# First layer's mixer in two halves of 256 tokens, the second half and no modulation chunk beside the first quarter of gathers

## The chip, the core and the metric

The kernel runs on one core of a Trainium2 chip. The core has TensorE (PE, matrix products into PSUM), VectorE (DVE), ScalarE (ACT), GpSimd (POOL) and SyncE (SP), which run their own instruction streams and meet at semaphores, and 16 DMA engines that serve several queues. Two queues matter here: SP's, which brings weights, and POOL's, which brings gathered rows. The metric is the device time of one launch in microseconds (us), as a median of runs.

## What is computed

A network of three layers over 512 tokens of width 1024, all in float32. Cut to what matters for the change:

```python
c_act = silu(c)
for l in range(2):
    mod = c_act @ ada_w[l] + ada_b[l]                     # 1024 x 6144
    sh1, sc1, g1, sh2, sc2, g2 = jnp.split(mod, 6, axis=-1)
    hn = modulate(rms_norm(h, norm_mix_g[l]), sh1, sc1)   # xn * (1 + scale) + shift
    mix = hgrn2_mixer(hn, ...) if l == 0 else stick_breaking_mixer(hn, k_sh, v_sh, ...)
    h = h + g1 * mix
    hn = modulate(rms_norm(h, norm_ffn_g[l]), sh2, sc2)
    h = h + g2 * peer_ffn(hn, ...)
    if l == 0:                                            # k_sh, v_sh; c_act @ kv_ada_w: 1024 x 2048
        k_sh, v_sh = shared_kv(h, c_act, ...)
h = rms_norm(h, final_norm_g)
# then second_block: convolution and windowed attention, then a mixture of 32 experts
```

`hgrn2_mixer` projects to q, f, i and g (1024 x 4096 weights), keeps a state of 128 x 128 in each of 8 heads, which goes from chunk to chunk of 16 tokens in order, and projects back with `w_out`. `peer_ffn` scores 2 x 128 subkeys in 4 heads, takes the best 64 experts of each token, and for each of them reads a row of 1024 numbers of `u` (a dot with the token gives the weight) and one of `v` (summed with these weights): 512 x 64 x 2 rows of 4 KB in each of the two layers.

## The kernel before

Tokens lie in four tiles of 128 (TT = 4). The program is a list of phases; all engines meet between two of them (`enter`, `leave`). The first seven phases hold the first layer up to its expert scores, for all four tiles at a time: `setup_*`, the norm, `hgrn_in_*` (projections), `hgrn_scan_*` (four levels of masked scores, then the state from tile to tile), `hgrn_out_norm_*`, the output projection with the second norm, and `peer_query`.

Then comes one long phase, `rows_pe`, `rows_act`, `rows_dve`, `rows_pool`. It has four quarters (w = 0 to 3) of 64 steps. A quarter serves two tiles: in steps 0 to 31 DVE takes the dots of the `u` rows (`dots_dve`, L943, four rows a step), in steps 32 to 63 PE sums the `v` rows (`sum_pe`, L1034). POOL gathers the rows (`gather_pool`, L931: 128 rows of 4 KB in one DMA) into a ring of 6 pairs of buffers, so it is at most three steps ahead. Beside it the quarters w = 1 and 2 run the second layer's mixer for half of the tokens each, as generators (`block_pe`, `block_act`, `block_dve`), of which every engine takes one piece at fixed steps (`seg_step`); w = 3 does so with the first half of the second block. Quarter w = 0 has no such block, but the last 18 of the modulation chunks. `route_dve` (the selection of 64 experts) of the odd tile runs in steps 1 to 11 of its own quarter, that of the next quarter's even tile late in the quarter before; that of tile 0 runs ahead of the first step.

A modulation chunk is a product of `c_act` (a column) with 1024 x 512 weights, 2 MB: there are 12 for each layer and 4 for `shared_kv`, 28 in all. `mod_parts_pe` (L242) multiplies it on PE in four groups of 32 columns, ACT copies the partial sums, `mod_total_pe` (L273, L275) adds bias and partial sums over all 128 partitions, ACT writes the result. Four chunks run in setup, six beside the projections of `hgrn_in_pe`, which load into a buffer of their own (`MOD_SIDE`), and 18 in the first quarter (`MOD_STEP`).

Weights of 1024 x 512 (2 MB) come on SP's queue through two slots, w0 and w1, in the order of `stream`. POOL also writes 13 MB of zeros to `x_slots`, which the last block needs (`zero_slots`), at the start of `hgrn_in`.

```python
MOD_EARLY = 10
MOD_FIRST = 4
MOD_STEP = {2 + 3 * j: j for j in range(len(MODS[1]))}
ROWS_AT, TURN_AT = (2, 16), (26, 40)
```

## Time and profile before

| | us |
|---|---|
| median of 3 runs | 3250.94 (3245.38 to 3251.22) |
| the profiled execution | 3263.15 |
| its span | 3261.6 |
| first-layer phases, to the copy ahead of the first dots | 0 to 569.3 |
| first quarter of gathers (w = 0) | 569.3 to 1017.9 |
| second quarter (w = 1) | 1017.9 to 1457.9 |
| third quarter (w = 2) | 1457.9 to 1906.9 |
| fourth quarter (w = 3) | 1906.9 to 2364.5 |
| the rest of the second block, and the experts | 2364.5 to 3261.6 |

The bounds of the quarters are the starts of the copies at L959, of tiles 0, 2, 4 and 6. The profile shows busy times of the engines, which don't add up to the span, since they overlap; what an engine waits for decides. PE was busy for 2242.1 us (69%), DVE for 1368.6 (42%), POOL for 1089.2 (33%), ACT for 482.3 (15%), and the DMA engines moved 963.65 MB, 295 GB/s over the span.

### The profile page before, as it was taken

Reading aid. Unit: us, or ns where it says so; the run is one execution under the profiler, and the core shown is the slowest. Engines: PE = TensorE matmul, PEld = TensorE weight load, DVE = VectorE, ACT = ScalarE, POOL = GpSimd, SP = SyncE. Lnnn points to the kernel's source line nnn. Section 1 sums busy time; section 2 is a strip of 40 time slices with the busy share of each in tenths; the row PEclk is TensorE's granted clock in tenths of the full one; section 3 lists DMA queues with packets and bytes.
Section 4 is the critical chain, followed back from the end, with each engine's and each line's share of the span. In section 5 each row is a group of like instructions: output and inputs, shape, how many; then the busy total and the mean of one; then the engine's idle time right before and its main releaser. Section 6 shows DMA issues by size and latency. Waiting matters only on the chain.

```text
span 3261.6 us, 27740 instructions
## 1 busy us (share of the span) xinstructions
PE 2242.1 (69%) x10176; PEld 1180.6 (36%) x10176; DVE 1368.6 (42%) x3001; ACT 482.3 (15%) x817; POOL 1089.2 (33%) x1220
## 2 busy tenths in 40 slices
PE   6999796323555657848577626667788758888884
PEld 2444543111113343405463315533377423333331
DVE  1032523785305962149661369683136211111112
ACT  2121211000001032101151010020022101111111
POOL 2000000564555546564555555466400010000001
PEclk8999898555777867968789758788899769898997
DMA  7542011999998989998989989999824278989995
GB/s 282 204 150 78 14 52 58 386 405 379 403 403 327 405 342 340 350 376 342 365 303 366 344 324 358 373 326 365 316 103 144 99 277 339 391 349 399 396 394 193
DMA packets 273994, 963.65 MB, mean 295 GB/s; under 512 B 31760, under 2 KB 36880, under 8 KB 261582
## 3 DMA queue, kind: packets, MB, share of 16 engines
q0 software_dynamic: 159728, 577.32, 46.8%
q1 hardware_dynamic: 102920, 378.61, 30.6%
q10 hardware_dynamic: 11222, 6.03, 0.7%
q8 instruction: 82, 1.34, 0.2%
q14 instruction: 42, 0.34, 0.0%
HBM read 933.30 MB, written 28.57 MB: 295 GB/s over the span
## 4 chain that ended last, share of the span: by engine, by line
PE 50%; DMA 12%; issue 11%; DVE 10%; another core or an unknown queue 6%; POOL 6%; ACT 4%; POOLq 0%; DVEq 0%; SPq 0%; ACTq 0%
PE psum L194 25%; PE psum L2080 8%; DMA arena<-in_peer_v_dram,arena 6%; POOL arena L931 5%; PE psum L2094 5%; PE psum L1034 4%; DMA arena<-in_peer_u_dram,arena 2%; DVE arena L943 2%; PE psum L1140 1%; DMA arena<-in_sb_w_q_dram 1%; DMA arena<-in_kv_w_dram 1%; PE psum L1430 1%; PE psum L242 1%; DMA arena<-in_ada_w_dram 1%
## 5 line engine op out<-in xcount | busy, mean ns | idle before, releaser
L194 PE MATMUL psum<-arena 128*128 128x256 f32 (+3 forms) x3144 | 974.1, 470 | 92.7 <-issue 35.5
L194 PEld LDWEIGHTS psum<-arena 128*128 128x128 f32 x3144 | 606.8, 198 | 469.5 <-issue 386.9
L931 POOL DMA_INDIRECT arena<-in_peer_u_dram,arena x512 | 485.6, 949 | 589.8 <-DVE arena L943 247.4
L931 POOL DMA_INDIRECT arena<-in_peer_v_dram,arena x512 | 502.8, 982 | 385.7 <-PE psum L1034 200.9
L943 DVE CUSTOM_DVE_ANT_0 arena<-arena,psum 128x1024 f32<-128x1024 f32 x512 | 594.1, 1217 | 44.0 <-DMA arena<-in_peer_u_dram,arena 29.4
L1034 PE MATMUL psum<-arena 128*32 128x512 f32 x2048 | 320.5, 757 | 222.9 <-DMA arena<-in_peer_v_dram,arena 188.8
L2080 PE MATMUL psum<-arena 128*64 128x512 f32 x1088 | 253.8, 621 | 67.0 <-issue 65.8
L1034 PEld LDWEIGHTS psum<-arena 128*32 128x32 f32 x2048 | 68.7, 126 | 424.8 <-issue 420.9
L2094 PE MATMUL psum<-arena 128*64 128x512 f32 x544 | 161.4, 748 | 17.6 <-DVE arena L2130 17.6
L2080 PEld LDWEIGHTS psum<-arena 128*64 128x64 f32 x1088 | 80.5, 142 | 239.3 <-issue 237.9
L2126 DVE TENSOR_TENSOR arena<-arena,psum 64x512 f32<-64x512 f32 x34 | 23.5, 692 | 313.6 <-ACT arena L2107 313.6
L2140 POOL DMA_DIRECT2D arena<-x_slots x37 | 19.1, 517 | 381.1 <-DVE arena L2114 373.6
L984 PE MATMUL psum<-arena 128*32 128x16 f32 x512 | 18.9, 203 | 156.0 <-issue 83.6
L242 PE MATMUL psum<-arena 128*32 128x512 f32 x448 | 76.9, 819 | 44.4 <-DMA arena<-in_kv_ada_w_dram 26.9
L1020 DVE TENSOR_TENSOR arena<-arena 128x512 f32<-128x512 f32 x32 | 21.8, 691 | 189.5 <-PE psum L1034 157.9
L2019 POOL DMA_INDIRECT x_slots<-arena x8 | 7.7, 967 | 275.0 <-DVEq L180 272.9
L1650 DVE SCALAR_TENSOR_TENSOR arena<-arena 128x256 f32<-128x256 f32 x240 | 97.4, 480 | 0.0
L2107 ACT ACTIVATE arena<-psum 64x512 f32<-64x512 f32 x34 | 20.0, 588 | 513.9 <-PE psum L2080 513.9
L1045 DVE TENSOR_TENSOR psum<-psum,arena 128x1024 f32<-128x1024 f32 x8 | 9.9, 1233 | 199.2 <-PE psum L1034 113.9
L1140 PE MATMUL psum<-arena 128*128 128x256 f32 (+1 forms) x208 | 56.2, 440 | 53.6 <-DVE arena L1283 39.9
L2156 POOL DMA_DIRECT2D x_slots<-arena x68 | 36.7, 540 | 149.2 <-DVE arena L2134 147.6
L2094 PEld LDWEIGHTS psum<-arena 128*64 128x64 f32 x544 | 45.0, 173 | 108.8 <-issue 86.5
(331 smaller groups left out, 2038.1 us busy)
## 6 DMA issues: line engine op xcount, KB each, us to landing
arena<-in_w_gate_dram SPq DMA_DIRECT2D x32, 2048.0 KB, 20.4
arena<-in_w_up_dram SPq DMA_DIRECT2D x32, 2048.0 KB, 9.9
arena<-in_w_down_dram SPq DMA_DIRECT2D x32, 2048.0 KB, 14.4
arena<-in_ada_w_dram SPq DMA_DIRECT2D x24, 2048.0 KB, 7.9
arena<-in_w_in_dram SPq DMA_DIRECT2D x14, 2048.0 KB
arena<-in_hgrn_w_in_dram SPq DMA_DIRECT2D x8, 2048.0 KB
arena<-in_kv_w_dram SPq DMA_DIRECT2D x8, 2048.0 KB
x_slots<-arena POOLq DMA_DIRECT2D x25, 512.0 KB, 13.9
```

Of the source, the lines that this page charges most:

```text
L194: last = pe.matmul(o, lhsT=lhs(k), rhs=rhs(k), start=start and k == 0, stop=stop and k == n - 1)
L242: last = pe.matmul(bank(MOD_BANKS[l][0], 0, 512, parts=(32 * q, 32)), lhsT=C_COLS(k0 + q), rhs=w[:, k0 + q, :], start=k0 == 0, stop=k0 == ...
L931: pool.indirect_dma_start(RING(n, k), None, (U_TAB, V_TAB)[v], bass.IndirectOffsetOnAxis(ap=at, axis=0))\
L943: last = dve.tensor_tensor_reduce(out=row, in0=row, in1=bank(XB0, 0, D), scale=1.0, scalar=0.0, op0=ALU.mult, op1=ALU.add, accum_out=par_s ...
L1034: last = pe.matmul(bank(ACC + half, 0, 512, parts=(32 * g, 32)), lhsT=mem("t", D + (s // 4 % 2) * 512 + (g * GR + s % 4) * 32, 32), rhs=RI ...
L1140: last = pe.matmul(bank(ZB(h), o + w - min(w, wm), min(w, wm)), lhsT=mem("negtri" if m == n else "negones", 0, P), rhs=AW(hf, h, om, wm), ...
L1430: last = pe.matmul(bank(b, p * 256, 256, parts=(64 * a, 64)), lhsT=wslot(i)[:, k, a * 256 + (2 * b + p) * 64:a * 256 + (2 * b + p) * 64 + 64],
L1650: ins = dve.scalar_tensor_tensor(Y2(hf, c), CV(c, 256 * hf + i, 256), CCOL(c, i), Y2(hf, c), ALU.mult, ALU.add)
L2080: last = pe.matmul(bank(2, 0, FF, parts=half(m)), lhsT=XBT[:, k, :], rhs=EW(e, m)[:, k, :], start=k == 0, stop=k == KD - 1, skip_group_che ...
L2094: last = pe.matmul(bank(4, 0, 512, parts=half(n)), lhsT=HT[:, k, :], rhs=EW(e, 2)[:, k, n * 512:(n + 1) * 512], start=k == 0, stop=k == NF ...
L2126: dve.tensor_tensor(HM, SG, bank(2, 0, FF, parts=half(1)), ALU.mult).then_inc(sem("hm"), 1)
L2156: pool.dma_start(y_slots[bass.ds(g * SLOTS, SLOTS), m * 512:(m + 1) * 512], mem("w1", 0, D // 2, parts=half(m)))\
```

## The change

The seven phases are gone: after `setup_*` there is the long phase alone. The first layer's mixer, the second norm and the expert scores become a generator of 36 pieces (`first_pe`, `first_act`, `first_dve`), which works on two tiles. Half 0 (tiles 0 and 1) runs ahead of the quarters, half 1 (tiles 2 and 3) beside the first quarter at the steps of `first_step`. All 28 chunks run beside half 0: four ahead of its first piece, and one after each of its first 24 pieces on PE. POOL loads them (`mods_pool`) into two buffers, in r5 and r6, and puts one block of zeros for `x_slots` behind each. A chunk that is needed as a row over the width (g1, sh2, sc2, g2 of both layers: 16 chunks) goes by way of DRAM: DVE adds its bias (`mod_out_dve`), POOL stores 2 KB of it, waits until they have landed, and later reads the row back for all partitions. POOL does this in one stream with the loads. The partial sums of a chunk are copied by DVE (`mod_acc_dve`), no longer by ACT, and are added on PE with a weight of a single column (L654) or, for the other 12 chunks, in four products with one column each (L657). The weights of the first layer's mixer are read twice, once for each half. The biases and gains that are needed as columns are loaded in setup: 72 columns of 128 numbers, 4 bytes a piece. The expert scores of tiles 2 and 3 are there only at step 51 of the first quarter, so the selection for tile 2 moves from step 36 to step 53. The quarters w = 1, 2 and 3 keep their work; w = 1 gains four loads of rows (`rows_1_act`), and the window constants move on POOL to the start of w = 2.

```diff
-        add("mod0", [w_cols(ada[0], 512 * j) for j in range(MOD_FIRST)])
-        add("hgrn_in", [w_cols(win[0], D * part + 512 * c) for part in (1, 0, 2, 3) for c in range(2)])
-        add("hgrn_out", [w_cols(A["hgrn_w_out"][0], 512 * c) for c in range(2)])
-        add("peer_q0", [w_cols(A["peer_w_q"][0], 512 * c) for c in range(2)])
-        add("mod1", [w_cols(ada[0], 512 * j) for j in range(MOD_EARLY, 12)] + [w_cols(kva, 512 * j) for j in range(4)] + [w_cols(ada[1], 512 * j) for j in range(12)])
+        for hf in range(2):
+            add(f"hgrn_in{hf}", [w_cols(win[0], D * part + 512 * c) for part in (1, 0, 2, 3) for c in range(2)])
+            add(f"hgrn_out{hf}", [w_cols(A["hgrn_w_out"][0], 512 * c) for c in range(2)])
+            add(f"peer_q0{hf}", [w_cols(A["peer_w_q"][0], 512 * c) for c in range(2)])
+            add(f"keys0{hf}", [A["peer_subkeys"][0].rearrange("h p n d -> n (h p) d")])
...
+            for at, n, row in ((0, 16, A["kv_ada_b"]), (16, 16, A["ada_b"][1, 0:2 * D]), (64, 16, A["ada_b"][0, 0:2 * D]),
+                               (32, 8, A["kv_norm_g"]), (40, 8, A["norm_mix_g"][1]), (80, 8, A["norm_mix_g"][0])):
+                act.dma_start(mem("tiny", at, n), row.rearrange("(k p) -> p k", p=P), allow_slow_non_contiguous=True)\
+                    .then_inc(sem("cols_in"), 16)
+            act.dma_start(mem("r0", 0, 2 * D, parts=(0, 1)), A["norm_ffn_g"].rearrange("(a l) n -> a (l n)", a=1))\
+                .then_inc(sem("cols_in"), 16)
...
+        def mods_pool(pool):
+
+            for j in range(2, NCHUNK + 4):
+                i = j - 4
+                if i in ROW_NO:
+                    r = rows_before(i) + 1
+                    pool.wait_ge(sem("mod_row"), r)
+                    pool.dma_start(mod_rows[ROW_NO[i] // 2:ROW_NO[i] // 2 + 1, 512 * (i % 2):512 * (i % 2) + 512], MOD_ROW(i))\
+                        .then_inc(sem("mod_stored"), 16)
+                    pool.wait_ge(sem("mod_stored"), 16 * r)
+                    n = ROW_NAMES[ROW_NO[i] // 2]
+                    if i % 2 and n[-2:] == "_0":
+                        pool.dma_start(mod(MOD0[n[:-2]]), mod_rows[ROW_NO[i] // 2:ROW_NO[i] // 2 + 1, :].broadcast_to([P, D]))\
+                            .then_inc(sem("row_g2" if n == "g2_0" else "row_in"), 16)
+                if j < NCHUNK:
+                    pool.wait_ge(sem("mod_acc"), j - 1)
+                    mod_load(pool, j)
+                    if j in ROW_NO:
+                        pool.dma_start(MOD_ROW(j), mod_source(j)[1]).then_inc(sem(f"mod_bias{j % 4}"), 16)
+                zero_slots(pool, j - 2)
...
+        def mod_acc_dve(dve, j, link):
+
+            if j >= 2:
+                dve.wait_ge(sem("mod_mm"), j - 1)
+            if BY_PE[j]:
+                dve.wait_ge(sem("mod_part"), sum(BY_PE[:j + 1]))
+                dve.tensor_copy(MOD_ACC(j), bank(6 + j % 2)).then_inc(sem("mod_acc"), 1)
+                return
...
+
+            if not BY_PE[j]:
+                return
+            mod_arrived(pe, j)
+            if j >= 2:
+                pe.wait_ge(sem("mod_acc"), j - 1)
+            for k0 in (0, 4):
+                for q in range(4):
+                    last = pe.matmul(bank(6 + j % 2, 0, 512, parts=(32 * q, 32)), lhsT=C_COLS(k0 + q), rhs=MOD_W(j)[:, k0 + q, :],
+                                     start=k0 == 0, stop=k0 == 4, skip_group_check=True)
+            last.then_inc(sem("mod_part"), 1)
+
...
+        def mod_sum_pe(pe, j):
+
+            pe.wait_ge(sem("mod_acc"), j + 1)
+            if j >= 2:
+                pe.wait_ge(sem("mod_out"), j - 1)
+            over = FIRST_OF_32 if BY_PE[j] else mem("ones", 0, 1)
+            if j in ROW_NO:
+                last = pe.matmul(bank(4 + j % 2, 0, 512, parts=(0, 1)), lhsT=over, rhs=MOD_ACC(j), start=True, stop=True)
+            else:
...
+            first = marks[f"hgrn_in{hf}"]
+            on_act("x7")
+            for i in range(4):
+                project_pe(pe, first, i, lambda k: head("X", k), did)
+                yield
+            for i in range(4):
+                on_act(f"f{i}")
+                project_pe(pe, first + 2, i, lambda k: head("X", k), did)
+                yield
+            for i in range(4):
+                on_act(f"q{i}")
+                by_token_pe(pe, first + 4, i, lambda k, o, n: head("X", k, o, n), did)
+                yield
...
+        first_step = lambda i: (1 if i == 0 else 2 + int((i - 1) * 1.4) if i < 17 else 25 + int((i - 17) * 2.1) if i < 24
+                                else 39 + int((i - 24) * 1.15))
...
-        ROUTES = {(0, 1): (1, 0.9), (0, 2): (36, 0.9), (1, 3): (1, 0.9), (1, 4): (53, 0.5), (2, 5): (1, 0.9), (2, 6): (53, 0.5), (3, 7): (1, 0.9)}
...
+            if w == 0:
+                return sum(first_step(i) == s for i in range(A_SEGS))
+            return sum(seg2_step(i) == s for i in range(SEGS2))
+        ROUTES = {(w, 2 * w + 1): (1, 0.9) for w in range(4)} | {(w, 2 * w + 2): (53, 0.5) for w in range(3)}
...
         def rows_pe(pe):
-            block = iter(())
+            for j in range(4):
+                mod_parts_pe(pe, j)
+                if j:
+                    mod_sum_pe(pe, j - 1)
+            mod_sum_pe(pe, 3)
+            for s, _ in enumerate(first_pe(pe, 0)):
+                if 4 <= s + 4 < NCHUNK:
+                    mod_parts_pe(pe, s + 4)
+                if 4 <= s + 2 < NCHUNK:
+                    mod_sum_pe(pe, s + 2)
             for w in range(TILES // 2):
                 a, b = 2 * w, 2 * w + 1
+                if w == 0:
+                    block = first_pe(pe, 1)
                 if w in (1, 2):
                     block = block_pe(pe, w - 1)
...
-                    if w == 0 and s in MOD_STEP:
-                        mod_pe(pe, 1, [MOD_STEP[s]])
...
         def rows_dve(dve):
             link = linker(dve, "dve")
+            block = first_dve(dve, 0, link)
+            next(block)
+            for j in range(4):
+                mod_acc_dve(dve, j, link)
+                if j:
+                    mod_out_dve(dve, j - 1, link)
+            mod_out_dve(dve, 3, link)
+            for s in range(1, A_SEGS):
+                if s + 3 < NCHUNK:
+                    mod_acc_dve(dve, s + 3, link)
+                if 4 <= s + 1 < NCHUNK:
+                    mod_out_dve(dve, s + 1, link)
+                next(block)
             for _ in route_dve(dve, 0, link):
                 pass
-            block = iter(())
             routes = {}
             for w in range(TILES // 2):
                 a, b = 2 * w, 2 * w + 1
+                if w == 0:
+                    block = first_dve(dve, 1, link)
                 if w in (1, 2):
...
-        phase(**norm(0, mod(MOD0["sc1"]), mod(MOD0["sh1"]), xn_temp, "r0"))
-        phase(hgrn_in_pe, hgrn_in_act, hgrn_in_dve, hgrn_in_pool)
-        phase(hgrn_scan_pe, hgrn_scan_act, hgrn_scan_dve, hgrn_scan_pool)
-        phase(hgrn_out_norm_pe, hgrn_out_norm_act, hgrn_out_norm_dve, window_pool)
-        o0 = out_proj(0, marks["hgrn_out"], lambda k, t: FM("r2", k, t * P, P), KD, MOD0["g1"])
-        n1 = norm(1, mod(MOD0["sc2"]), mod(MOD0["sh2"]), lambda t: mem("r0", t * D, D), "r1", ready=o0["ready"])
-        phase(*both(o0, n1, before=lambda act: peer_load_keys(act, 0)))
-        phase(**peer_query(0))
```

Three places in the order of instructions. The first is PE in the first layer's input projections. Of before, one chunk of the modulation and one 2 MB piece of the projection's weights: L273 and L275 add up the chunk before, L242 multiplies the next, L194 are the projections for 512 tokens.

```order
L273 MATMUL psum<-arena 128x512 [waits mod_bias0,mod_out]
L275 MATMUL psum<-arena 128x512 [waits mod_part]
L242 MATMUL psum<-arena 32x512 [waits mod_side,mod_part]
L242 MATMUL psum<-arena 32x512 x7
L194 MATMUL psum<-arena 128x512 [waits f_out,w_ready0]
L194 MATMUL psum<-arena 128x512 x7
L194 MATMUL psum<-arena 128x512 [waits f_out]
L194 MATMUL psum<-arena 128x512 x7
L194 MATMUL psum<-arena 128x512 [waits f_out]
L194 MATMUL psum<-arena 128x512 x7
L194 MATMUL psum<-arena 128x512 [waits f_out]
L194 MATMUL psum<-arena 128x512 x7
```

Now the same place, with 256 tokens: L188 are the projections, L643 the product of a chunk, L654 its sum over the partitions.

```order
L188 MATMUL psum<-arena 128x256 [waits w_ready0,a_act]
L188 MATMUL psum<-arena 128x256 x15
L643 MATMUL psum<-arena 32x512 [waits mod_acc,mod_w1]
L643 MATMUL psum<-arena 32x512 x7
L654 MATMUL psum<-arena 1x512 [waits mod_out,mod_acc]
L188 MATMUL psum<-arena 128x256 [waits a_act]
L188 MATMUL psum<-arena 128x256 x15
L643 MATMUL psum<-arena 32x512 [waits mod_acc,mod_w0]
L643 MATMUL psum<-arena 32x512 x7
L654 MATMUL psum<-arena 1x512 [waits mod_out,mod_acc]
```

A chunk stood behind 32 products of 512 columns; it stands behind 16 of 256 now. The sum with 128 weight columns and its bias product (two instructions) is one product with one weight column.

The second place is POOL ahead of its first gather. Of before, the zeros for `x_slots` in one go (L1924), and then the constants of the scan.

```order
L1924 DMA x_slots<-arena 128x1024 [waits left_dve,left_pool,left_act,left_pe]
L1924 DMA x_slots<-arena 128x1024 x24
L1924 DMA x_slots<-arena 64x1024
L622 MEMSET arena 128x1024 [waits left_dve,left_pool,left_act,left_pe]
L622 MEMSET arena 128x1024 x3
L623 MEMSET arena 128x384
```

Now the loads of chunks 8 to 11. L588 loads a chunk, L615 its bias, L1904 writes zeros, L604 stores 2 KB of a finished row, L609 reads two such pieces back for all partitions.

```order
L604 DMA mod_rows<-arena 16x1x32 [waits mod_row]
L588 DMA arena<-in_ada_w_dram 128x8x512 [waits mod_acc,mod_stored]
L615 DMA arena<-in_ada_b_dram 1x16x32
L1904 DMA x_slots<-arena 128x1024
L604 DMA mod_rows<-arena 16x1x32 [waits mod_row]
L609 DMA arena<-mod_rows 128x1024 [waits mod_stored]
L588 DMA arena<-in_ada_w_dram 128x8x512 [waits mod_acc]
L615 DMA arena<-in_ada_b_dram 1x16x32
L1904 DMA x_slots<-arena 128x1024
```

A load of a chunk now stands behind the store of the row that was finished two chunks earlier, and behind its landing (`mod_stored`).

The third place is DVE at step 11 of the first quarter. Of before, dots alone (L943, each with the read of its sum).

```order
L943 ISA arena<-arena,psum 128x1024 [waits ring2]
L943 ISA arena 128x1
L943 ISA arena<-arena,psum 128x1024
L943 ISA arena 128x1
L943 ISA arena<-arena,psum 128x1024 [waits ring3]
L943 ISA arena 128x1
L943 ISA arena<-arena,psum 128x1024
L943 ISA arena 128x1
```

Now the prefix sums of the second half of the mixer stand between the dots (L449) of two steps: L934 is 1 - f, L935 the prefix sum, L936 a copy of the last values of each chunk of 16 tokens.

```order
L934 TENSOR_SCALAR arena<-arena 128x512 [waits a_act]
L935 SCALAR_TENSOR_TENSOR arena<-arena 128x512
L936 COPY arena<-arena 128x32 [waits chain_dve]
L934 TENSOR_SCALAR arena<-arena 128x512 [waits a_act]
L935 SCALAR_TENSOR_TENSOR arena<-arena 128x512
L936 COPY arena<-arena 128x32 [waits chain_dve]
L934 TENSOR_SCALAR arena<-arena 128x512 [waits a_act]
L935 SCALAR_TENSOR_TENSOR arena<-arena 128x512
L936 COPY arena<-arena 128x32 [waits chain_dve]
L934 TENSOR_SCALAR arena<-arena 128x512 [waits a_act]
L935 SCALAR_TENSOR_TENSOR arena<-arena 128x512
L936 COPY arena<-arena 128x32 [waits chain_dve]
```

DVE waits there for ACT's logarithms (`a_act`), and the dots behind it wait with it.

## Rows read from the trace of the kernel before

**Rows 1.** windows: us, busy us of PE, PEld, DVE, ACT, POOL, clock, DMA share, GB/s

```profile
0.00:64.50 64.50, 36.59 (x112) 12.64 (x112) 12.31 (x16) 19.44 (x33) 6.91 (x30) 0.79 0.72 251
64.50:314.00 249.50, 246.92 (x632) 103.47 (x632) 44.00 (x72) 46.66 (x81) 13.87 (x26) 0.99 0.44 159
314.00:381.00 67.00, 54.08 (x440) 52.05 (x440) 42.01 (x77) 8.07 (x14) 5.89 (x14) 0.92 0.09 32
381.00:400.00 19.00, 7.11 (x16) 2.96 (x16) 11.60 (x17) 15.91 (x27) 1.48 (x3) 0.80 0.09 28
400.00:473.00 73.00, 65.19 (x160) 30.81 (x160) 21.51 (x29) 11.36 (x21) 0.00 (x0) 0.90 0.19 65
473.00:541.00 68.00, 65.90 (x200) 33.03 (x200) 0.00 (x0) 10.77 (x19) 0.00 (x0) 0.97 0.17 62
541.00:570.00 29.00, 0.44 (x33) 0.47 (x37) 28.01 (x112) 1.77 (x3) 0.00 (x0) 0.58 0.09 19
570.00:790.00 220.00, 57.21 (x327) 28.34 (x319) 180.79 (x378) 8.87 (x19) 131.74 (x140) 0.55 1.02 397
790.00:1018.00 228.00, 131.84 (x752) 37.85 (x752) 38.45 (x130) 13.15 (x24) 120.73 (x127) 0.75 1.01 391
1018.00:1240.00 222.00, 130.00 (x542) 97.23 (x543) 187.00 (x395) 47.47 (x75) 120.98 (x128) 0.75 0.93 355
1240.00:1458.00 218.00, 155.28 (x828) 68.09 (x827) 49.65 (x146) 26.02 (x47) 124.10 (x129) 0.81 0.95 353
```

**Rows 2.** timeline, start: three rows, start us, length us, engine, [idle before <-releaser]

```profile
30.42 0.37 SPq L147 DMA_DIRECT2D arena<-in_ada_w_dram  x1
38.28 3.64 PE L242 MATMUL psum<-arena 128*32 128x512 f32 x16 [2.42 <-DMA arena<-in_ada_w_dram]
53.95 1.94 PE L447 MATMUL psum<-arena 128*128 128x128 f32 x8 [8.02 <-DVE arena L434]
```

**Rows 3.** DMA packets in 3 to 5 us, then in 7 to 13 us

```profile
DMA packets 1787, 0.33 MB, mean 166 GB/s; under 512 B 1628, under 2 KB 1628, under 8 KB 1787
DMA packets 2035, 2.13 MB, mean 355 GB/s; under 512 B 1018, under 2 KB 1018, under 8 KB 2035
```

**Rows 4.** DMA issues: engine, count, KB each, median us from issue to landing

```profile
arena<-in_x_dram ACTq DMA_DIRECT2D x1, 2048.0 KB, 18.9
arena<-in_hgrn_onorm_g_dram ACTq DMA_DIRECT2D x1, 4.0 KB, 11.2
arena<-x_slots POOLq DMA_DIRECT2D x2, 2.0 KB, 4.1
```

**Rows 5.** timeline of PE at the full clock, and beside gathers

```profile
574.43 1.13 PE L275 MATMUL psum<-arena 128*128 128x512 f32 x2
575.49 1.92 PE L242 MATMUL psum<-arena 128*32 128x512 f32 x16
1035.29 27.89 PE L194 MATMUL psum<-arena 128*128 128x256 f32 x128 [0.90 <-ACT arena L1202]
1068.02 29.62 PE L194 MATMUL psum<-arena 128*128 128x512 f32 x64 [4.84 <-DMA arena<-in_kv_w_dram]
```

**Rows 6.** timeline of DVE, first layer: one prefix sum, one tile of one level

```profile
194.90 1.22 DVE L580 TENSOR_TENSOR_SCAN arena<-arena 128x512 f32<-128x512 f32 x1
346.70 1.35 DVE L711 COPY_PREDICATED arena<-arena,psum 128x512 f32<-128x512 int32 x2
347.94 0.68 DVE L715 TENSOR_TENSOR arena<-arena 128x512 f32<-128x512 f32 x1
348.54 0.69 DVE L716 TENSOR_TENSOR arena<-arena 128x512 f32<-128x512 f32 x1
```

**Rows 7.** timeline of DVE: the first selection begins, the first dots

```profile
541.34 1.64 DVE L853 MAX8 arena<-arena 128x8 f32<-128x128 f32 x8 [70.63 <-ACTq L180]
569.33 1.22 DVE L959 COPY psum<-arena 128x1024 f32<-128x1024 f32 x1
577.53 1.22 DVE L943 CUSTOM_DVE_ANT_0 arena<-arena,psum 128x1024 f32<-128x1024 f32 x1 [6.98 <-DMA arena<-in_peer_u_dram,arena]
```

1133 lines of the change are left out of this document (525 added, 608 removed).

## The prediction

> **What bounds the kernel now.** I read the windows by stage first, because the change moves whole stages [rows 1]. Nothing is gathered until 569.3 us. From 64.5 to 314 PE is busy for 246.92 of 249.5 us at a granted clock of 0.99: the input projections are bound by PE at its upper level (2.4 GHz), and DMA is at 0.44. From 314 to 381 the levels of the scan go back and forth between PE and DVE; from 381 to 400 it is the output norm, with ACT; from 400 to 541 the output projection, the second norm and the queries, PE again. DVE alone selects until 570. In the first quarter DMA is the bound in both parts: 397 and 391 GB/s at a share of 1.02 and 1.01. In the second quarter, which has a mixer beside the gathers, DMA has 355 and 353 GB/s, and DVE is busy for 187.00 of 222 us in the part with the dots. So two prices are needed: that of half a mixer with 28 chunks beside it, and that of half a mixer beside the first quarter.
>
> **Setup.** In setup ACT now also loads 72 columns in 4-byte pieces, 72 x 128 = 9,216 of them, behind x, and the phase ends only when they are there. Small pieces alone went at 1,628 in 2 us, 814 per us; beside the 2 MB loads on SP's queue at 1,018 in 6 us, 170 per us [rows 3]. The old columns land at 2.3 + 11.2 = 13.5 us, and x, which had its last byte at 23.2 us behind 512 KB that are gone, about 21.5 [rows 4]. SP now issues four 2 MB loads at once (two chunks, two pieces of weights), 8.4 MB. Beside small pieces 2.13 MB passed in 6 us, 0.35 per us [rows 3], so 2.9 MB by 13.5; beside x, whose pieces are 4 KB against 2, a third of 400 GB/s, 1.0 more by 21.5. The other 4.5 last until about 34.5, and 2,200 small pieces pass beside them. The last 7,000 need 8.6 us. The long phase begins at **43 us**; 35 to 75 are the ends (all small pieces at 814 or at 170 per us).
>
> **First four chunks.** Squares, roots and scaling of the norm take 5 us (before, with one more operation, PE waited for them for 8.02), two products 3.64 each at the lower level of the clock (1.2 GHz), [rows 2]. POOL issues the third load when the first sum is copied, at about 49. A load alone was multiplied 7.9 us after its issue [rows 2]; the fourth lands behind it and behind 512 KB of zeros, 6.6 us later (2.6 MB at 397 GB/s): 63.5. Product, copy, sum and addition bring 71, turns and ACT's copies 75, the fifth product 78. The first projection starts at **78 us**, against 64.5 [rows 1].
>
> **Sixteen projection pieces.** A piece is 16 products of 256 columns: 64 took 27.89 us [rows 5], so 7.0. A chunk adds 1.92 (L242 at the upper level) and a sum of 1.13 (L275) [rows 5], and some 0.4 of starts: 10.5. DMA needs 2.1 MB of chunk, 0.52 of zeros and 1.05 of weights in it, 9.3 us at 397 GB/s. That is close, but hides. For eight of the sixteen, the load of a later chunk stands behind a stored row: 4.1 us for a 2 KB transfer of POOL's queue [rows 4], 7.9 for the load, 1.3 for the zeros ahead of the next store, 13.3 in a row. Part of the latency overlaps with the product's own turn; the ends are 10.5 and 15.9 (SP's 1.05 MB wholly in series), and I take 12.8. Sum: 8 x 10.5 + 8 x 12.8 = 186, to **264 us**. The Trainium skill's page DMA: Bandwidth & Descriptors, section Anatomy of one DMA — SWDGE (gpsimd) path, gives a fixed 2.0 us and 436 GB/s for a transfer of this queue; by it store, load and zeros would last 10.0 us, PE's 10.5 would decide throughout, and the kernel would end some 25 us earlier than I forecast. The 4.1 us above were longer than that.
>
> **Scan and output norm.** One tile of one level was 1.35 us of masks and 2 x 0.6 of decay, 2.56 from one tile to the next [rows 6]; two tiles, the chunk's copy and its addition make 6.2 on DVE, and the first product of the next level is in the open: 8.5. Three pieces of 8.5, 4 for ACT's four gates ahead of them (an estimate: four operations of 512 columns and a change of function), then four pieces whose chunks again stand behind stored rows, 12 each, and 5 in which the output norm (19 us for four tiles, [rows 1]) outlasts the last chunk: 82.5, to **346 us** (ends -15 and +25).
>
> **Tail and selection.** Output projection to scores took 73 + 68 us for four tiles [rows 1]; half of it is 70.5. What doesn't halve is the chain behind the last product (addition, square, root, scaling, turn, copy), the turn of the keys, and two sums of chunks; I take 9.5 for it, 80 in all, with ends at 76 and 92. I add 5 for stretches at the lower level of the clock after the scan. Selection: 28.0 [rows 7]. The copy ahead of the dots comes at 346 + 80 + 5 + 28 = 459, say **460**, in place of 569.3: **-109 us**.
>
> **First quarter.** It loses 18 chunks, and gains half a mixer with its 12 loads of 2 MB and one of 0.5 MB. Steps 0 to 31: the second quarter is the nearest. Its 187.0 us of DVE less some 9 of its own mixer are 178. Half of the first mixer costs on DVE: eight turns of one tile and level at 2.56 less the decay of the first two, 18; prefix sums 4 x 1.45, 6; twenty operations of 512 columns at 0.6, 12; gates, norm, fill and decay products 7 [rows 6]: 43. With 8 us until the first rows are there (569.33 to 577.53, [rows 7]) and 20 of waits for ACT and PE between dots, this is 249, against 221 before. Is PE late? Beside gathers PE waits for weights (4.84 us at 1068.02, [rows 5]); eight pieces of 2 MB at about 17 us each end near 150 us into the quarter, ahead of DVE's step 24. DMA needs 67 MB of rows and some 21 of weights, 222 us at 397 GB/s, so DVE decides by a little. Steps 32 to 63: 218 us as in the second quarter, against 228, since the chunks' 20 MB are gone. Sum **+20 us**; the ends are 0 (all of DVE's extra work in DMA's shadow) and +60 (each of the 36 pieces costs a wait of over a microsecond on top).
>
> **Others.** Four row loads in w = 1, 2.1 MB, 5 us of DMA half hidden: +2. The work that leaves ACT and the single phase bounds are in the numbers above. The quarters w = 2 and 3 and all behind them keep their times.
>
> **Sum.** -109 + 20 + 2 = **-87 us**. Against its own 3263.15 the profiled execution would be 3176; the median lies 12 below it, so I forecast 3250.9 - 87 = **3164 us**.
>
> **Rivals.**
> 1. PE at its lower level through half 0. Before, it was at 0.99 because it hardly waited; beside waits for loads it was 0.75 to 0.81 [rows 1]. If the waits behind stored rows pull it down throughout, a piece is 14.0 + 3.64 + 2.1 = 19.7 us in place of 11.7, +128 in sixteen pieces and +56 in the tail's two projections: the end is about 3350, slower. It decides from about half of the stretch on. Against it: PE will be busy for 10.1 of 10.5 to 12.8 us, 79 to 96%, and where it was busy for 54.08 of 67 and 65.19 of 73 us before, the clock was 0.92 and 0.90. The Trainium skill's page TensorE: Matmul & The Clock Gate, section HAM oscillation — how this bites in real kernels, tells of a kernel that waits for each slice of weights, and in which the clock falls in every wait, so that the next slice starts slow. This has 0.03.
> 2. The first quarter pays for all: DVE's in-order waits empty the ring at each piece, +80 in place of +20, and the time is 3224. DVE was idle for 35 of 222 us in w = 1 [rows 1], which speaks for some of it; that PE is ahead of DVE by the sum above speaks against. It has 0.05 above my range.
> 3. Loads never show (10.5 us throughout, setup at 36), and the quarter's extra DVE work is hidden: -109 - 18 - 16 - 7 with +2 is -148, 3103. Nothing excludes it, but all three terms must be at their ends: 0.08 below my range.
> 4. The half mixer moves work but frees nothing: DVE and DMA in the quarter take what the start gives. For no change the first quarter would have to be 107 us longer than its 448.5 [rows 1], 555 us; its 134 MB of rows and 27 of weights would then pass at 290 GB/s, and no part of a quarter was under 353 [rows 1]. It has 0.02.
>
> **How the numbers follow.** The ends of the terms are setup -8 and +32, pieces -18 and +25, scan -15 and +25, tail -4 and +12, quarter -20 and +40; they hardly fall together, and a root of squares is -32 and +64, of which I take most: **3115 to 3218**, with 0.80 in it. Below it 0.08, above it but faster 0.05, within 0.2% (6.5 us, about what a measurement of this kernel can tell from no change) 0.02, slower 0.05 (rival 1, and 0.02 for a first quarter beyond 555 us). Faster: 0.93.
>
> **What would show it.** In the changed kernel: the first L643 at 43 us, the first L188 at 78, its pieces 10.5 us apart while chunks 5 to 7 and the columns' chunks are loaded and near 13 between; the last masks at about 330; the first gather at 460; DMA under 350 GB/s in steps 0 to 31, and 218 us for the sums. I would be wrong if PE's clock is near 0.5 to 0.8 before 250 us, if the pieces are over 14 us apart, or if the first quarter is over 500 us.

## The result, and the profile after

The changed kernel takes 3141.10 us (median of 4 runs, 3136.08 to 3147.05) where the kernel before took 3251.08 (3245.38 to 3252.50) on the same chip: a ratio of 0.9666, 95% interval 0.9643 to 0.9688, which is 110 us faster. I had forecast 3164 with 3115 to 3218. The profiled execution took 3143.82 us (span 3142.3), 119.3 less than that of before (3263.15); the terms below add up to this number. It is larger than 110 because the profiled execution of before lay 12 us above its median, that of the changed kernel 3 above.

The windows of the changed kernel, cut where a stage of the prediction ends. Columns as in [rows 1].

```profile
0.00:40.50 40.50, 0.00 (x0) 0.00 (x0) 0.54 (x3) 2.98 (x4) 8.69 (x40) 1.00 0.90 260
40.50:76.20 35.70, 25.52 (x128) 12.62 (x128) 5.49 (x14) 9.11 (x16) 7.15 (x10) 0.67 0.77 276
76.20:266.50 190.30, 167.60 (x781) 100.95 (x777) 42.10 (x78) 22.08 (x36) 34.01 (x52) 0.93 0.87 311
266.50:336.10 69.60, 56.33 (x366) 32.55 (x366) 36.29 (x65) 14.07 (x20) 14.50 (x23) 0.88 0.71 259
336.10:412.70 76.60, 65.94 (x252) 43.98 (x252) 13.71 (x20) 12.29 (x28) 1.47 (x3) 0.96 0.27 93
412.70:440.70 28.00, 0.00 (x0) 0.00 (x0) 27.35 (x112) 5.46 (x9) 0.00 (x0) 0.51 0.18 66
440.70:684.00 243.30, 149.50 (x704) 116.48 (x704) 218.17 (x449) 29.10 (x48) 134.61 (x139) 0.80 0.95 362
684.00:896.60 212.60, 160.01 (x872) 74.28 (x872) 59.70 (x165) 28.42 (x49) 121.15 (x126) 0.84 0.96 361
896.60:1338.80 442.20, 289.56 (x1368) 169.58 (x1368) 236.50 (x541) 73.77 (x122) 246.67 (x260) 0.79 0.93 352
1338.80:3142.30 1803.50, 1289.30 (x6152) 713.83 (x6152) 753.22 (x1635) 272.77 (x458) 572.37 (x628) 0.85 0.83 313
```

The starts of two quarters, from the timeline of DVE (the copy ahead of the first dots of tiles 0 and 2; before, 569.33 [rows 7] and 1017.9):

```profile
440.67 1.22 DVE L467 COPY psum<-arena 128x1024 f32<-128x1024 f32 x1
896.56 1.22 DVE L467 COPY psum<-arena 128x1024 f32<-128x1024 f32 x1
```

The copy comes 128.7 us earlier (forecast 109). The first quarter is 455.9 us long where it was 448.5 (+7.4, forecast +20), the second 442.2 where it was 440.0 (+2.2, forecast +2). From there to the end it is 1803.5, and was 1803.7. So -128.7 + 7.4 + 2.2 - 0.2 = -119.3. Nothing behind the second quarter took part.

What [rows 5] showed of the kernel before as one sum (1.13), one chunk's product (1.92) and projections is now this, from the timeline of PE (L188 projections, L643 a chunk, L654 its sum), and beneath it from that of POOL in the same 26 us (L604 stores 2 KB of a row, L588 loads a chunk, L1904 writes zeros):

```profile
104.80 7.17 PE L188 MATMUL psum<-arena 128*128 128x256 f32 x32
111.90 1.92 PE L643 MATMUL psum<-arena 128*32 128x512 f32 x16
113.64 1.02 PE L654 MATMUL psum<-arena 128*1 128x512 f32 x2
114.59 7.17 PE L188 MATMUL psum<-arena 128*128 128x256 f32 x32
127.58 3.64 PE L643 MATMUL psum<-arena 128*32 128x512 f32 x16 [5.81 <-DMA arena<-in_ada_w_dram]
130.99 1.91 PE L654 MATMUL psum<-arena 128*1 128x512 f32 x2
```

```profile
106.47 0.50 POOL L604 DMA_DIRECT2D mod_rows<-arena  x1 [2.56 <-DVE arena L667]
112.32 0.55 POOL L609 DMA_DIRECT2D arena<-mod_rows  x1 [5.34 <-DMA mod_rows<-arena]
112.87 0.98 POOL L588 DMA_DIRECT2D arena<-in_ada_w_dram  x1
113.84 0.51 POOL L615 DMA_DIRECT2D arena<-in_ada_b_dram  x1
114.34 0.57 POOL L1904 DMA_DIRECT2D x_slots<-arena  x1
116.27 0.50 POOL L604 DMA_DIRECT2D mod_rows<-arena  x1 [1.36 <-DVE arena L667]
129.26 0.94 POOL L588 DMA_DIRECT2D arena<-in_ada_w_dram  x1 [12.49 <-DMA mod_rows<-arena]
```

A piece without a wait is 9.79 us from one L188 to the next. With a wait it is 18.25: 5.81 of idle PE, then the chunk in 3.64 and its sum in 1.91 in place of 1.92 and 1.02, since the granted clock has fallen to its lower level (0.50) in the wait. The load that PE waits for was issued at 112.87, behind the store of 106.47, whose landing POOL waited for. The next store (2 KB, 116.27) is waited for 12.49 us: it is in the same queue as the 2 MB load and the 512 KB of zeros issued 2 to 3 us before it, and lands when these have: the zeros 14.5 us after their issue at 114.34, the store 12.7 after its own at 116.27, at 128.8 and 129.0.

### The profile page after: what moved, and what is told of

Same layout as the page of the kernel before. It is cut to its first block, busy times and chain, and to the rows that moved or that the text cites. A ratio compares the mean times of both kernels' runs of the same rounds, so it can differ in the third digit from the quotient of the medians.

```text
span 3142.3 us, 28617 instructions
## 1 busy us (share of the span) xinstructions
PE 2203.8 (70%) x10616; PEld 1264.3 (40%) x10616; DVE 1393.1 (44%) x3073; ACT 470.1 (15%) x789; POOL 1140.6 (36%) x1278
## 4 chain that ended last, share of the span: by engine, by line
PE 43%; DVE 14%; DMA 13%; issue 13%; another core or an unknown queue 7%; POOL 4%; ACT 4%; ACTq 1%; POOLq 0%; PEldq 0%; DVEq 0%; SPq 0%; PEld 0%
PE psum L188 20%; PE psum L2060 8%; DVE arena L449 5%; PE psum L2074 4%; DMA arena<-in_peer_v_dram,arena 4%; PE psum L542 4%; POOL arena L437 4%; DVE arena L1606 2%; DMA arena<-in_ada_w_dram 2%; DMA mod_rows<-arena 1%; PE psum L643 1%; PE psum L1162 1%; DMA arena<-in_kv_w_dram 1%; DMA arena<-in_w_down_dram 1%
## 5 line engine op out<-in xcount | busy, mean ns | idle before, releaser
L188 PE MATMUL psum<-arena 128*128 128x256 f32 (+4 forms) x3656 | 987.1, 430 | 102.4 <-issue 32.6
L188 PEld LDWEIGHTS psum<-arena 128*128 128x128 f32 x3656 | 707.7, 199 | 397.9 <-issue 278.1
L437 POOL DMA_INDIRECT arena<-in_peer_v_dram,arena x512 | 510.4, 997 | 376.3 <-PE psum L542 188.1
L449 DVE CUSTOM_DVE_ANT_0 arena<-arena,psum 128x1024 f32<-128x1024 f32 x512 | 593.2, 1217 | 27.3 <-issue 12.0
L542 PE MATMUL psum<-arena 128*32 128x512 f32 x2048 | 312.0, 740 | 184.3 <-DMA arena<-in_peer_v_dram,arena 153.8
L643 PE MATMUL psum<-arena 128*32 128x512 f32 x448 | 73.0, 785 | 86.4 <-DVEq L174 40.6
L731 PE MATMUL psum<-arena 128*128 128x128 f32 x128 | 25.1, 379 | 93.1 <-DVE arena L922 50.5
```

The costliest lines, as they stand in the source:

```text
L188: last = pe.matmul(o, lhsT=lhs(k), rhs=rhs(k), start=start and k == 0, stop=stop and k == n - 1)
L437: pool.indirect_dma_start(RING(n, k), None, (U_TAB, V_TAB)[v], bass.IndirectOffsetOnAxis(ap=at, axis=0))\
L449: last = dve.tensor_tensor_reduce(out=row, in0=row, in1=bank(XB0, 0, D), scale=1.0, scalar=0.0, op0=ALU.mult, op1=ALU.add, accum_out=par_s ...
L542: last = pe.matmul(bank(ACC + half, 0, 512, parts=(32 * g, 32)), lhsT=mem("t", D + (s // 4 % 2) * 512 + (g * GR + s % 4) * 32, 32), rhs=RI ...
L643: last = pe.matmul(bank(6 + j % 2, 0, 512, parts=(32 * q, 32)), lhsT=C_COLS(k0 + q), rhs=MOD_W(j)[:, k0 + q, :], start=k0 == 0, stop=k0 == ...
L731: last = pe.transpose(bank(b, (k % 2) * 256 + i * P, P), src(i, k), ident)
```

## The experiments

The chips differ: on the three of the experiments the kernel before took 3185 to 3190 us. So each run is read by its ratio to the kernel before on its own chip. The changed kernel was run again on one of them only, that of e5, e6 and e7; e1 to e4 ran on another, and e1 again, e8, e9 and e10 on the third. A difference between one of these and the repeated kernel is one across chips. The stage times are from the profiles: *pieces* is from the first L188 to the first product of the levels, *scan* from there to the first product of the output projection, *copy* the start of the first quarter.

### The changed kernel again

> The changed kernel again, on the chip of this group of runs, so that the others of the group have a ratio beside theirs on the same chip. Both theories: the ratio to the kernel before is 0.965 to 0.968. If the ratio depends on the chip (the last four runs were on one on which the kernel before took 3185 us and a quarter about 25 us less), it lies apart: the start is bound by PE and by waits, which don't shrink on such a chip, so the part gained is larger, 0.960 to 0.965.

Ratio 0.9617 (0.9589 to 0.9644), 3059.34 us against 3184.85: 125 us. First L188 at 73.8, pieces 186.2, scan 69.9, copy at 434.8, first quarter 437.1. The ratio lies where the second guess puts it, though its interval touches that of the first chip. The other runs that leave the sixteen pieces of half 0 alone (e2, e3, e5) took 187.4, 186.2 and 191.8 us for them and 70.3, 70.6 and 70.5 for the scan, so these stages repeat within some 6 us.

### e1: POOL waits for a stored row behind the next load

```diff
                     pool.dma_start(...)  (the store of the row)
-                    pool.wait_ge(sem("mod_stored"), 16 * r)
-                    ...  (read back for all partitions)
                 if j < NCHUNK:
                     pool.wait_ge(sem("mod_acc"), j - 1)
                     mod_load(pool, j)
+                if i in ROW_NO:
+                    pool.wait_ge(sem("mod_stored"), 16 * r)
+                    ...  (read back for all partitions)
```

> POOL issues a row's store as in the changed kernel, then the load of the next chunk, and only then waits for the store to land, reads the row back and loads the bias. Theory A: the load of a chunk is late because POOL waited 5 to 12 us for a 2 KB store that stands in its own queue behind the 2 MB load and the 512 KB of zeros before it. Then PE's waits for chunk loads between 76 and 336 us (10 of them, some 41 us in all, with 8 to 10 us more from the lower clock behind them) mostly go: the copy ahead of the first dots comes at about 400 in place of 440.7, and the time is 3100 (3141 - 40). Theory B: these waits are the DMA engines' own limit (share 0.88 from 114.6 to 264 us): the loads land as late as before, the copy stays within 8 us of 440.7, and the time is 3133 to 3143.

Ratio 0.9522 (0.9501 to 0.9544). The copy is at 402.8. The same stretch as above, from the timelines of PE and of POOL (L645 and L656 are the chunk and its sum here):

```profile
104.85 7.17 PE L188 MATMUL psum<-arena 128*128 128x256 f32 x32
111.95 1.92 PE L645 MATMUL psum<-arena 128*32 128x512 f32 x16
113.69 1.02 PE L656 MATMUL psum<-arena 128*1 128x512 f32 x2
114.64 7.17 PE L188 MATMUL psum<-arena 128*128 128x256 f32 x32
121.75 1.92 PE L645 MATMUL psum<-arena 128*32 128x512 f32 x16
```

```profile
106.53 0.50 POOL L604 DMA_DIRECT2D mod_rows<-arena  x1 [3.80 <-DVE arena L669]
107.02 0.95 POOL L588 DMA_DIRECT2D arena<-in_ada_w_dram  x1
110.22 0.54 POOL L613 DMA_DIRECT2D arena<-mod_rows  x1 [2.26 <-DMA mod_rows<-arena]
```

The load goes out at 107.02 where it went out at 112.87, and the next chunk is multiplied at 121.75, not at 127.58. The windows over pieces and scan:

```profile
76.30:237.90 161.60, 157.91 (x781) 98.30 (x777) 41.99 (x78) 22.05 (x36) 33.76 (x52) 0.99 0.99 364
237.90:297.90 60.00, 50.54 (x366) 31.81 (x366) 36.30 (x65) 14.06 (x20) 14.46 (x23) 0.97 0.82 305
```

The pieces fall from 190.2 to 161.6 us at a clock of 0.99, the scan from 69.6 to 60.0. DMA, which had a share of 0.87 and 311 GB/s, gives 364 at 0.99. Theory B falls: the DMA engines were not the limit, they had been left without work. (First and repeated changed kernel were on other chips; their pieces, 190.2 and 186.2, are both far from 161.6.)

> The edit of e1 again (POOL waits for a stored row behind the next load), on the chip of this group, to tell how far its gain repeats. Both theories: a ratio to the kernel before of 0.948 to 0.953, the sixteen projection pieces in about 162 us, the copy ahead of the first dots at 400 to 405.

Ratio 0.9485 (0.9454 to 0.9516); pieces 159.4, scan 60.1, copy at 400.0. It repeats. That the gain is not the chips' is shown by e6 below, which holds this edit and ran on the chip of the repeated kernel: 0.9490 against 0.9617.

### e2: the columns in runs

```diff
-                act.dma_start(mem("tiny", at, n), row.rearrange("(k p) -> p k", p=P), allow_slow_non_contiguous=True)\
+                act.dma_start(mem("tiny", at, n), row.rearrange("(p k) -> p k", p=P))\
                     .then_inc(sem("cols_in"), 16)
```

> The 72 columns of biases and gains in setup are read as one run of 32 or 64 bytes for each partition (the numbers land in another order, so this leaves out the right assignment of biases), 6 x 128 pieces in place of 9,216. Theory A: the 4-byte pieces are what ends setup; the first chunk product comes at about 31 us in place of 40.5 and the time is 3132. Theory B: the four 2 MB loads of SP's queue end it (8.4 MB and 2 MB of x at 400 GB/s are 26 us, with 7 us of start 33): the first product still comes at 33 to 35 at the earliest, -6 us; if chunk 2's load, which POOL issues only after the first sum, decides in both, the whole of it passes through to the end unchanged.

The first chunk product comes at 31.90 us, not at 40.55, the copy at 430.4; ratio 0.9542 (0.9518 to 0.9565). Theory A holds for setup: 8.7 us are the small pieces', and four loads of 2 MB don't keep the phase over 31.9. At the copy 4.4 us of them are left (430.4 against 434.8), which is within what this point varies by. The ratio says more (0.0075, 24 us below the repeated kernel's, with 12 us of uncertainty) than the profiles do, whose executions took 3041.3 and 3046.0 us: that of the repeated kernel was the shortest of five that reach 3072.8. The kernel of this run leaves out the right assignment of the biases, other biases also choose other experts, so that the rows gathered are others, and I put no cause to the rest.

### e3: both halves ahead of the quarters

```diff
+            for _ in first_pe(pe, 1):
+                pass
             for w in range(TILES // 2):
-                if w == 0:
-                    block = first_pe(pe, 1)
...
```

and so on ACT and DVE; nothing of the block runs at the steps of w = 0.

> Half 1 of the mixer runs ahead of the first quarter too, and the first quarter has nothing beside it. Theory A (my sum): half 1 alone is 16 pieces of 7.2 us, some 50 of scan and norm and 75 of tail, about 240 us, and the quarter without it falls from 456 to about 395, since DVE loses 37 us of work and DMA 25 MB: the time is 3141 + 240 - 60 = 3320. Theory B (nothing is hidden in the quarter: DVE and DMA take what the start gave): the quarter falls to the 338 us that 134 MB take at 397 GB/s, and the time is 3265.

Ratio 1.0043 (1.0023 to 1.0062). The copy is at 635.8, 201 us later than the repeated kernel's (I had 240), and the first quarter lasts 370.4 in place of 437.1, 67 less (I had 60). Its two parts, from the windows:

```profile
635.80:834.00 198.20, 12.54 (x165) 11.09 (x163) 179.90 (x379) 7.10 (x14) 129.78 (x137) 0.54 0.96 371
834.00:1006.00 172.00, 89.98 (x544) 19.97 (x544) 36.88 (x126) 1.79 (x3) 122.95 (x128) 0.76 1.03 408
```

and those of the changed kernel, repeated on a chip that gives the same second quarter (411 and 413 us):

```profile
434.80:671.60 236.80, 147.46 (x704) 115.44 (x704) 217.66 (x448) 28.86 (x48) 133.68 (x138) 0.80 0.96 371
671.60:871.90 200.30, 149.89 (x872) 71.31 (x872) 60.29 (x167) 28.42 (x49) 122.51 (x128) 0.87 1.00 384
```

So half a mixer costs 201 us by itself and 39 + 28 us beside the gathers. In the first part DVE has 38 us more to do and the part is 39 longer, as it would be if DVE decides there. This run alone doesn't show it, since DMA moves 371 GB/s at a share of 0.96 in both, so that its added bytes would make the same 39 us; e5 tells the two apart. Theory B falls by its stages: the quarter lost 67 us, not the 118 that it asks for. By the time alone it would have stood, since its 3265 is 1.0043 of the 3251 that it was reckoned from, but only because half 1 alone cost 201 us where I had taken 240. The run says a second thing: with both halves ahead, and all chunks beside half 0, the kernel is 10 to 14 us slower than before (by the medians and by the ratio). What the change gains comes entirely from the half beside the gathers; halving the mixer and moving the chunks cost more than they gave.

### e4: the chunks on DVE

```diff
-        BY_PE = [True for j in range(NCHUNK)]
+        BY_PE = [False for j in range(NCHUNK)]
```

> All 28 chunks are multiplied on DVE (8 operations of 512 columns, some 5 us) in place of PE (1.92 us); PE only adds them up. Theory A (the loads decide): a chunk's buffer is held 3.3 us longer, which is added to each load that waits for it, in the first four chunks, the eight behind stored rows and in the scan, where DVE had 6.2 us of work in each piece of 8.5 and now has over 9: 40 us more, 3180. Theory B (PE decides in the sixteen projection pieces): a piece falls from 9.85 to 8.2 us and the time is 3141 - 15 = 3126.

Ratio 0.9646 (0.9615 to 0.9677), against 0.9617 (0.9589 to 0.9644): not to be told apart. The profile tells why both numbers failed: first L188 7.7 us later than the repeated kernel's (81.5), pieces in 176.4 (10 less), scan in 86.7 (17 more), copy at 451.2 (16 later, where the repeated kernel, the first chip and e5, with half 0 untouched, spread over 434.8 to 443.9). From its timeline of PE and then of DVE:

```profile
133.02 7.17 PE L188 MATMUL psum<-arena 128*128 128x256 f32 x32
147.54 1.87 PE L654 MATMUL psum<-arena 128*1 128x512 f32 x2 [7.34 <-DVEq L674]
149.34 7.85 PE L188 MATMUL psum<-arena 128*128 128x256 f32 x32
```

```profile
140.75 0.48 DVE L627 TENSOR_SCALAR arena<-arena 128x512 f32<-128x512 f32 x1 [8.88 <-DMA arena<-in_ada_w_dram]
141.27 5.47 DVE L629 SCALAR_TENSOR_TENSOR arena<-arena 128x512 f32<-128x512 f32 x7
```

DVE too waits for the load behind the stored row (8.88 us), and then needs 5.9 for the chunk. In the pieces PE's 1.9 us are saved wherever no load is late; in the scan, where DVE has work of its own, its chunks seem to be in the way (the scan is 17 us longer; no run tests DVE there by itself). That each chunk is multiplied on PE is worth nothing that the times can tell, though the profile's start is 16 us shorter with it.

### e5: the levels behind the dots

```diff
-        first_step = lambda i: (1 if i == 0 else 2 + int((i - 1) * 1.4) if i < 17 else 25 + int((i - 17) * 2.1) if i < 24
-                                else 39 + int((i - 24) * 1.15))
+        first_step = lambda i: (1 if i == 0 else 2 + int((i - 1) * 1.4) if i < 17 else 31 + i - 17
+                                )
```

> In the first quarter the four pieces with the levels of half 1 (steps 25 to 31) and all behind them run at steps 31 to 49. Theory A (DVE decides the part with the dots, where it is busy for 218 of 243 us, and has room in the part with the sums, 60 of 213): the dots take 15 us less, the sums up to 5 more, the time is 10 us less than the changed kernel's. Theory B (DMA decides both parts, at a share of 0.95 and 0.96): the dots' part gets shorter and the sums' longer by the same, the quarter stays within 4 us.

Ratio 0.9657 (0.9634 to 0.9680), 13 us above the repeated kernel's, with 12 us of uncertainty. The profile is clearer. The dots' part took 223.4 us in place of 236.8, as theory A has it, but the sums' part 226.8 in place of 200.3, which neither has. In the dots' part DVE was busy for 205.20 us, 12.5 less than in the repeated kernel, and DMA went at 385 GB/s where it had gone at 371: so DMA could have given more, and DVE had decided there.

```profile
443.90:667.30 223.40, 129.41 (x592) 98.94 (x592) 205.20 (x428) 28.86 (x48) 132.95 (x138) 0.78 0.99 385
```

The waits of POOL in the sums' part, of e5 and then of the repeated kernel (us in total, times, longest):

```profile
POOL arena L437 <- PE psum L542: 66.4, 20, 10.0
```

```profile
POOL arena L437 <- PE psum L542: 42.8, 13, 6.4
```

and two windows of 20 us of e5 in it:

```profile
724.00:744.00 20.00, 20.00 (x107) 7.59 (x109) 4.83 (x10) 0.00 (x0) 7.48 (x8) 1.00 0.71 255
784.00:804.00 20.00, 20.00 (x122) 13.52 (x122) 3.06 (x3) 2.40 (x6) 9.22 (x10) 1.00 0.81 266
```

PE is busy without a gap there, at the full clock, with pieces of the block ahead of the sums; the ring is not emptied, POOL waits 24 us more, and DMA falls to 255 GB/s. I had looked for room on DVE and DMA and not on the third engine.

### e6 and e7: columns asked for late, and with the levels of e5

```diff
-            for at, n, row in ((0, 16, A["kv_ada_b"]), (16, 16, A["ada_b"][1, 0:2 * D]), (64, 16, A["ada_b"][0, 0:2 * D]),
-                               (32, 8, A["kv_norm_g"]), (40, 8, A["norm_mix_g"][1]), (80, 8, A["norm_mix_g"][0])):
+            for at, n, row in ((64, 16, A["ada_b"][0, 0:2 * D]), (80, 8, A["norm_mix_g"][0])):
```

The other four are asked for behind ACT's first piece of half 0. Both runs also have the edit of e1.

> The edit of e1 (POOL waits for a stored row behind the next load), and 48 of the 72 columns of 4-byte pieces in setup are asked for only behind ACT's first piece of half 0, since no chunk before the 13th needs them. Theory A: the small pieces end setup, and two thirds of them are gone: the first chunk product comes at about 34 in place of 40.6, and the copy ahead of the first dots at 396 in place of 402.8: 6 us less than e1. Theory B: the small pieces only move, and slow the loads of the chunks and of the weights beside which they now pass: the first product is earlier, the copy is not.

Ratio 0.9490 (0.9467 to 0.9514). The first product comes at 35.33, not 40.6, but the copy at 402.1, as in e1 (402.8 and 400.0). The pieces took 169.0 us, not 161.6 or 159.4: the first of them that stands beside the small pieces waits, in the timeline of PE,

```profile
98.60 3.36 PE L644 MATMUL psum<-arena 128*32 128x512 f32 x16 [4.03 <-DMA arena<-in_ada_w_dram]
```

where e1 had no wait. Theory B for this run: the small pieces only moved. (In e10 the same edit did bring the copy forward; see there.)

> The edits of e5 and e6 together. Theory A: they add up, since they lie in stretches that don't touch: 3141 - 46 - 6 - 10, a ratio of 0.945 to the kernel before. Theory B: with the start shorter the first quarter is as it was, and the levels moved behind the dots collide with the sums: no better than e6.

Ratio 0.9535 (0.9514 to 0.9557): theory B, as e5 has shown it. The dots' part 223.1 us, the sums' 223.7, and 0.0045 (14 us) worse than e6.

### e8, e9 and e10: zeros last, sixteen chunks on DVE, all

```diff
             for j in range(2, NCHUNK + 4):
                 ...
-                zero_slots(pool, j - 2)
+            for i in range(N_CLEAR):
+                zero_slots(pool, i)
```

> e1, and POOL issues the 26 blocks of zeros (13 MB) behind the last chunk in place of one behind each chunk. Theory A: with e1 PE decides in the projections (9.8 us a piece, clock 1.00), though DMA is at a share of 0.99 to 1.03, so that 8 MB less there change nothing; the remaining 21 us of waits for chunk loads, mostly in the scan, halve, and the copy comes 8 us earlier than in e1. Theory B: the zeros, all at the end, stand ahead of the last row's store and of the weights of the output projection and the queries, which have a DMA share of only 0.3 to use; the start is as long as in e1 or longer.

Ratio 0.9451 (0.9422 to 0.9481), the lowest of all; pieces 157.2 us (e1 on the same chip 159.4), scan 55.3 (60.1), copy at 392.8 (400.0). The window of the pieces is PE's alone now, with DMA at 0.89:

```profile
73.20:230.40 157.20, 156.22 (x780) 98.13 (x777) 42.01 (x78) 22.20 (x37) 24.91 (x36) 1.00 0.89 324
```

Theory A holds in the profile, 7 us. By the ratios e8 and e1 (0.9485) can't be told apart.

For e9 `BY_PE` is false for chunks 4 to 19; e10 adds the late columns.

> e8, and the 16 chunks beside the projections are multiplied on DVE. Theory A: PE decided there, so a piece falls from 9.8 towards 8.2 us (7.15 of projections and 1.0 for the sum), where DMA needs 7.9 for its 3.15 MB: the sixteen pieces in 135 to 145 us, the copy 18 to 25 us earlier than in e8. Theory B: DVE holds a chunk's buffer for 5 us in place of 1.9, which is in the chain of load, product and next load of two buffers (8 + 5 + 1 us for every two pieces' loads is enough only if DVE is free at once; it does the gates' products and prefix sums in order ahead of it): a piece stays at 9.8 to 10.5.

> e9 with the late columns of e6. Theory A (small pieces end setup): 5 us less than e9. Theory B (as e6 showed, the columns only move: the first product came 5 us earlier and the copy did not): within 3 us of e9.

Ratios 0.9456 (0.9423 to 0.9490) and 0.9458 (0.9428 to 0.9489). In e9 the third to the seventh piece last 8.05 us each, as theory A has it, and the eighth to the fifteenth 7.8 to 14.3, mostly over 9, as B has it. In the tenth, four prefix sums stand ahead of the chunk on DVE, and PE's sum of it, at 160.41, comes after 5.42 us of waiting. The last of the sixteen projections still ends at 215.0, 142.4 us behind the start of the first, which is in theory A's range. In all it is 161.1 us, 4 more than with the products on PE, because of what follows, where PE takes the chunks back:

```profile
228.34 3.64 PE L647 MATMUL psum<-arena 128*32 128x512 f32 x16 [13.34 <-DMA arena<-in_ada_w_dram]
```

POOL could issue this load only at 216.03, when DVE was done with the buffer, so what the pieces had gained is lost in one wait. The copy of e9 is at 396.5. e10 has its first product at 36.0, the same 161.1 us of pieces and its copy at 389.4, 7 us earlier: in the profiles the late columns did bring something here, as theory A has it, where in e6 they had not. The times, with ratios that are 0.0002 apart, can't tell.

## Why the prediction was right

The direction and its cause held: e3 shows that the whole gain is half a mixer that costs 67 us beside gathers in place of 201. The terms miss by more than the time does: the profiled execution was forecast at 3176 and took 3144, 32 us less, and in the medians the miss is 23 (3164 and 3141), because I had taken the profiled execution to lie 12 us above the median, and it lies 3 above. By the terms:

| term | forecast, us | measured, us |
|---|---|---|
| setup, to the first chunk product | 43 | 40.5 |
| first projection at | 78 | 76.2 |
| sixteen projection pieces | 186 | 190.3 |
| scan and output norm | 82.5 | 69.6 |
| output projection to scores | 80 + 5 | 76.6 |
| selection | 28 | 28.0 |
| copy ahead of the dots | 460 (-109) | 440.7 (-128.7) |
| first quarter | +20 | +7.4 |
| second quarter | +2 | +2.2 |
| the rest | 0 | -0.2 |

**Setup** was right, and for its reason: without the small pieces it would be 31.9 (e2, forecast 34.5), so they cost 8.7 us (forecast 8.6).

**The sixteen pieces** have nearly the sum that I gave, by two errors that cancel. I took 12.8 us for each of eight pieces with a load behind a stored row, and 10.5 for the others. Measured, four pieces are at 15.8 to 18.5 and the others between 9.0 and 11.3, the most at 9.8. The step that failed in its size is the 2 KB store at 4.1 us, from [rows 4]: between the chunks' loads the eight waits for it were 4.6 to 12.5 us, since there it follows the load and the zeros of its own queue; seven of the eight landed within 0.2 us of these zeros. The row of before was no such store: it is the middle of two reads of 2 KB in the last block, 6.6 and 1.7 us. Behind the last chunk, with no load of their queue under way, three stores landed after 1.6, 1.5 and 5.0 us. As the prediction says, the Trainium skill (page DMA: Bandwidth & Descriptors, section Anatomy of one DMA — SWDGE (gpsimd) path) gives such a transfer a fixed 2.0 us; these eight waits are all above that, and 10.5 us throughout was not reached. e1 shows what the wait in its place costs: 29 us of the pieces (25 against the repeated kernel), 10 of the scan.

**Scan and output norm** was the largest miss of half 0, -12.9. I had DVE decide at 8.5 us a piece. On PE two of the four pieces with levels last 6.5 us:

```profile
266.46 3.82 PE L785 MATMUL psum<-arena 128*128 128x128 f32 x32
270.21 1.92 PE L643 MATMUL psum<-arena 128*32 128x512 f32 x16
272.07 1.05 PE L657 MATMUL psum<-arena 128*128 128x1 f32 x8
272.98 3.82 PE L785 MATMUL psum<-arena 128*128 128x128 f32 x32
```

The levels' products of the next piece run while DVE does the masks of this one, so PE's 3.8 + 1.9 + 1.1 decide, and my "first product of the next level in the open" was not there; the other two wait for loads. That hardly changed the sum, though: the fourth of these pieces starts 24.5 us behind the first, where three of 8.5 are 25.5. The miss lies elsewhere: the 4 us for ACT's gates did not show (PE goes from the last projection's chunk to the levels without a wait), the output norm did not outlast the last chunk by 5, and the four pieces behind stored rows took 45.2 us and not 48.

**The tail** was -8.4: the 5 us for a low clock were not used (0.96), and what doesn't halve was 6 and not 9.5 (76.6 less 70.5). **The clock** (rival 1): 0.93 in the pieces, 0.88 in the scan. Behind each of the eight waits of 2.2 to 6.1 us the chunk took 3.2 to 3.64 us in place of 1.92, at or near the lower level, but the next projection piece had its 7.2 us back, or at most 8.6, so rival 1's fall throughout did not come. By the rule weighed for it (the Trainium skill, page TensorE: Matmul & The Clock Gate, section HAM oscillation — how this bites in real kernels) the slice behind a wait starts slow, and the trace agrees: the chunk at 127.58 took 3.64 us.

**The first quarter**: the dots' part is 242.6 us (forecast 249), DVE's work there +36 (181.44 to 217.47 from the copy to the last dot; forecast +43). The sums' part is 213 (forecast 218), some 16 less than before. Each of these was taken 5 to 6 us too high; the mechanism, DVE in the first part, is shown by e3 and e5 together. Two of the signs did not come: DMA moved 362 GB/s in steps 0 to 31 and not under 350, and the last masks were at 296 us and not 330. Rival 2 (80 us more) and rival 4 fall with it. Rival 3 had its sign right for the start and the quarter; it needed loads that never show, to which only e1 and what is built on it come near.

**What stays open**: why e2's ratio is lower than its profile explains, why the late columns brought the copy forward in e10 and not in e6, and how the 9 us between executions in the start come about (434.8 to 443.9 for the same half 0).

## What to carry to other kernels

When work is put beside a long stretch that another engine or the DMA engines bound, price it by what the busiest engine of each part gets more, all three of them: 38 us more on DVE made 39 us, and pieces moved from there to where DVE was idle gave back 13 us and cost 26, where PE had stretches without a gap. A small store issued behind a large transfer in the same queue landed behind it here, so whatever waited for it waited for the large one too: issue the next load first and wait afterwards (here one moved wait was worth 1.0 to 1.4%, a quarter to a third of what the whole rewrite gave). A sum can be right with its terms wrong; look at single pieces, not at the stage.
